# Hybrid HGRN2, RG-LRU and MoE block on one core: moving the convolution's leading product, shortening GELU's argument and reordering the gate matmuls

## What is computed

```python
proj = h @ w_in + b_in
q, f_pre, v, g_out, lru_x, lru_g, gate_hg, gate_lru = split(proj)
y_hg = hgrn2_mixer(q, f_pre, v, g_out, lb, norm_g)          # S_t = diag(f_t) S_{t-1} + (1-f_t) v_t^T, o_t = S_t^T q_t
y_lru = rg_lru(causal_depthwise_conv(lru_x, conv_w, conv_b), ...) * gelu(lru_g)
merged = sigmoid(gate_hg) * y_hg + sigmoid(gate_lru) * y_lru
h = layer_norm(alpha * h + merged @ w_out)
h = layer_norm(alpha * h + shared_swiglu(h) + routed_experts(h))   # 64 experts, 6 per token
```

## Time and profile before

| | us |
|---|---|
| median of three runs | 1241.81 |
| lowest and highest | 1236.87, 1247.73 |
| profiled execution, its own time | 1246.69 |
| its span, first to last instruction | 1244.5 |
| PE busy | 1142.2 (92%) |
| PE's weight loads busy (beside the matmuls) | 737.9 (59%) |
| DVE busy | 764.5 (61%) |
| ACT busy | 426.9 (34%) |
| POOL busy | 205.3 (17%) |
| mean granted clock of TensorE | 0.977 |

### The profile page before, as it was taken

How to read it: one execution, slowest core, us unless ns; L and a number is a source line. 1 busy time by engine, 2 the same in 40 slices (tenths; PEclk the granted TensorE clock), 3 DMA queues, 4 the chain that set the end, 5 groups by cost and what they waited for, 6 DMA issues and landing times. The chain is left out here.

```text
span 1244.5 us, 17998 instructions
## 1 busy us (share of the span) xinstructions
PE 1142.2 (92%) x6336; PEld 737.9 (59%) x6336; DVE 764.5 (61%) x1276; ACT 426.9 (34%) x667; POOL 205.3 (17%) x109
## 2 busy tenths in 40 slices
PE   4999999999999999999899889989999989999991
PEld 4888878787879797456344444444444444444440
DVE  7748687878687777754535445544455535555558
ACT  6656564746565565011022121111111212112220
POOL 1524242433333333000000000000000000000000
PEclk9999999999999999999999899999999989999996
DMA  5303030303031203093669899998999989999923
GB/s 222 121 21 121 20 139 0 139 0 139 0 139 38 101 34 135 28 391 148 240 259 421 358 414 374 396 403 359 418 384 383 422 354 422 412 417 405 410 101 118
DMA packets 48291, 292.57 MB, mean 235 GB/s; under 512 B 7680, under 2 KB 9088, under 8 KB 16528
## 3 DMA queue, kind: packets, MB, share of 16 engines
q1 hardware_dynamic: 42944, 272.92, 54.1%
q0 software_dynamic: 5328, 19.40, 4.3%
HBM read 288.10 MB, written 4.19 MB: 235 GB/s over the span
## 5 line engine op out<-in xcount | busy, mean ns | idle before, releaser
L366 PE MATMUL pair<-hT,w_parts 128*128 128x264 f32 (+1 forms) x2112 | 378.3, 339 | 2.8 <-DVE hT L635 2.4
L366 PEld LDWEIGHTS pair<-hT,w_parts 128*128 128x128 f32 x2112 | 321.5, 189 | 49.3 <-issue 5.4
L1276 PE MATMUL pair<-raw,xgT 128*64 128x512 f32 x1088 | 239.2, 592 | 0.0
L1373 DVE TENSOR_TENSOR acc<-acc,pair 128x512 f32<-128x512 f32 x280 | 171.7, 680 | 78.6 <-PE pair L1301 78.5
L216 POOL TENSOR_TENSOR w_parts<-w_raw,w_parts 128x1024 fp32r<-128x1024 f32 x66 | 166.9, 2530 | 316.2 <-ACT w_parts L210 301.1
L1276 PEld LDWEIGHTS pair<-raw,xgT 128*64 128x64 f32 x1088 | 78.2, 137 | 155.2 <-issue 155.2
L850 POOL DMA_INDIRECT xg<-h_rows,idx x37 | 34.8, 942 | 678.1 <-DVE idx L844 678.1
L1309 PE MATMUL pair<-raw,aT 128*64 128x512 f32 x544 | 124.2, 598 | 0.0
L1348 ACT ACTIVATE y_hi<-pair,w_now 128x512 fp32r<-128x512 f32 x70 | 48.1, 687 | 216.3 <-PE pair L1309 215.4
L1300 PE MATMUL pair<-y_hi,ST 128*128 128x512 f32 x280 | 118.1, 422 | 1.6 <-DVE y_lo L1382 1.6
L1364 DVE TENSOR_TENSOR act_a<-act_s,pair 128x256 f32<-128x256 f32 x35 | 14.7, 421 | 169.7 <-ACT act_s L1341 169.7
(11 more groups left out here) (266 smaller groups left out, 1204.4 us busy)
## 6 DMA issues: line engine op xcount, KB each, us to landing
raw<-in_w_gate_up SPq DMA_DIRECT2D x136, 1024.0 KB, 9.8
raw<-in_w_down SPq DMA_DIRECT2D x68, 1024.0 KB, 8.3
w_raw<-in_w_in SPq DMA_DIRECT2D x36, 1024.0 KB, 6.7
first<-in_w_gate_up SPq DMA_DIRECT2D x4, 1024.0 KB, 11.7
xin<-in_x SPq DMA_DIRECT2D x4, 512.0 KB, 5.3
ws_gu<-in_ws_gate_up SPq DMA_DIRECT2D x1, 2048.0 KB, 7.7
h_rows<-acc SPq DMA_DIRECT2D x4, 512.0 KB, 21.1
first<-in_w_down SPq DMA_DIRECT2D x2, 1024.0 KB, 10.1
```

The lines of the kernel that those rows point to most:

```text
L366: last = pe.matmul(o, w[:, n % PARTS, pw, k * P:(k + 1) * P], hT[ph][:, k, of], start=(k == 0 and m == 0), stop=(k == KB - 1 and m == 2))
L1276: last = pe.matmul(GU[half[s], :], xgT[b][:, (KB // 2) * c + k, half[s]], w[s][:, k * 2 * F:(k + 1) * 2 * F], start=(c == 0 and k == 0), s ...
L1373: v.tensor_tensor(part, part, SUM[g % len(SUM)], ALU.add).then_inc(sem("sum_free"), 1)
```

## The change

Three edits in the mixer. ACT makes the first product of the convolution (`w3*x + cb`) right behind `xr`, with a semaphore of its own (`xc_begun`), and DVE adds the other three taps. GELU's argument is `(x^2 + 1/GELU_A) * x`, in a square and one `scalar_tensor_tensor`, and the factor GELU_A goes into the scale of ACT's sigmoid. On PE the transpose of the meta tokens' `k_st` comes first and has a semaphore of its own (`ktm_done`, `ktm_taken`), the two wide gate matmuls come ahead of the two narrow ones, and only the narrow ones wait for `ktm_taken`.

```diff
--- before.py
+++ after.py
@@ -278,7 +278,7 @@
         of_half = lambda bank: bank[:, 0:TT * CHUNK].rearrange("p (t s) -> p t s", t=TT)
         chunked = lambda t: t.rearrange("p (c s) -> p c s", c=NCH)
 
-        per_head = ("f_done q_done v_done vt_done x_done o_done l_done hg_done lru_done kt_done ri_done sc_done "
+        per_head = ("f_done q_done v_done vt_done x_done o_done l_done hg_done lru_done ktm_done kt_done ri_done sc_done "
                     "kv_done out_done rms_done").split()
         pe_sem = {n: sem("pe_" + n) for n in per_head}
 
@@ -391,14 +391,17 @@
 
 
                     pe.wait_ge(sem("kst_ready"), j + 1)
+                    pe.transpose(B7[0:META, 256:384], k_st[:, 0:META], ident[:]).then_inc(pe_sem["ktm_done"], 1)
                     for t in range(TT):
-                        pe.transpose(B4[:, t * P:(t + 1) * P], k_st[:, META + t * P:META + (t + 1) * P], ident[:])
-                    pe.transpose(B7[0:META, 256:384], k_st[:, 0:META], ident[:]).then_inc(pe_sem["kt_done"], 1)
+                        last = pe.transpose(B4[:, t * P:(t + 1) * P], k_st[:, META + t * P:META + (t + 1) * P], ident[:])
+                    last.then_inc(pe_sem["kt_done"], 1)
                     pe.wait_ge(sem("xc_ready"), j + 1)
                     pe.wait_ge(sem(f"lw_here_{s}"), 16 * r + 16)
-                    pe.wait_ge(sem("kt_taken"), j + 1)
                     for i, bank in enumerate((B5, B6)):
                         pe.matmul(bank[:, 0:T], lw[s][:, i], xc[:, META:TA], start=True, stop=True)
+
+                    pe.wait_ge(sem("ktm_taken"), j + 1)
+                    for i in range(2):
                         last = pe.matmul(B7[:, 32 + 16 * i:48 + 16 * i], lw[s][:, i], xc[:, 0:META],
                                          start=True, stop=True)
                     last.then_inc(pe_sem["ri_done"], 1)
@@ -528,14 +531,18 @@
                     for of, bank in zip(split_at, wide[GX]):
                         last = act.activation(xr[:, 3 + of.start:3 + of.stop], bank[:, 0:TA // 2], ACT.Identity, bias=c(C_BX))
                     last.then_inc(sem("x_taken"), 1)
+                    act.wait_ge(sem("x_taken"), j + 1)
+                    act.activation(xc[:], xr[:, 3:3 + TA], ACT.Identity, scale=c(C_W3), bias=c(C_CB))\
+                       .then_inc(sem("xc_begun"), 1)
                     split_hi(act, j, 7)
                     act.wait_ge(pe_sem["o_done"], j + 1)
                     act.activation(sg[0][:], BV_[:, 0:T], ACT.Silu, bias=c(C_BG)).then_inc(sem("o_taken"), 1)
                     split_hi(act, j + 1, 0)
                     act.wait_ge(pe_sem["l_done"], j + 1)
                     act.activation(gx[:], BQ_[:, 0:T], ACT.Identity, bias=c(C_BL)).then_inc(sem("l_taken"), 1)
+                    act.wait_ge(pe_sem["ktm_done"], j + 1)
+                    act.activation(kTm[:], B7[0:META, 256:384], ACT.Copy).then_inc(sem("ktm_taken"), 1)
                     act.wait_ge(pe_sem["kt_done"], j + 1)
-                    act.activation(kTm[:], B7[0:META, 256:384], ACT.Copy)
                     act.activation(kT[:].rearrange("p t c -> p (t c)"), B4[:, 0:T], ACT.Copy).then_inc(sem("kt_taken"), 1)
                     split_hi(act, j + 1, 1)
 
@@ -546,7 +553,7 @@
                     act.activation(ii[:, META:TA], B6[:, 0:T], ACT.Sigmoid, bias=c(C_BI)).then_inc(sem("ri_taken"), 1)
                     act.wait_ge(sem("ri_taken"), j + 2)
                     act.wait_ge(sem("gelu_arg"), j + 1)
-                    act.activation(gt[:], gt[:], ACT.Sigmoid, scale=GELU_B).then_inc(sem("gelu_sig"), 1)
+                    act.activation(gt[:], gt[:], ACT.Sigmoid, scale=GELU_A * GELU_B).then_inc(sem("gelu_sig"), 1)
                     act.activation(la[:], rr[:], ACT.Exp, scale=own[s][:, 2:3])
                     act.activation(pp[:], rr[:], ACT.Tanh, scale=own[s][:, 3:4]).then_inc(sem("a_ready"), 1)
                     act.wait_ge(pe_sem["hg_done"], j + 1)
@@ -565,7 +572,7 @@
 
         @block.vector
         def _(v):
-            N = 38
+            N = 36
             st0 = Steps(v, sem("dve2_step"))
             st0.add(v.memset(ones[:], 1.0))
             st0.add(v.memset(k_in[:], 0.0))
@@ -682,8 +689,7 @@
                         else:
                             ins.then_inc(sem("qk_ready"), 1)
 
-                    v.wait_ge(sem("x_taken"), j + 1)
-                    st(v.tensor_scalar(xc[:], xr[:, 3:3 + TA], c(C_W3), c(C_CB), ALU.mult, ALU.add))
+                    v.wait_ge(sem("xc_begun"), j + 1)
                     for i in range(3):
                         ins = v.scalar_tensor_tensor(xc[:], xr[:, i:i + TA], c(C_W0 + i), xc[:], ALU.mult, ALU.add)
                         if i < 2:
@@ -692,8 +698,8 @@
                             ins.then_inc(sem("xc_ready"), 1)
                     v.wait_ge(sem("l_taken"), j + 2)
                     st(v.tensor_tensor(gt[:], gx[:], gx[:], ALU.mult))
-                    st(v.tensor_scalar(gt[:], gt[:], GELU_A, 1.0, ALU.mult, ALU.add))
-                    v.tensor_tensor(gt[:], gt[:], gx[:], ALU.mult).then_inc(sem("gelu_arg"), 1)
+                    v.scalar_tensor_tensor(gt[:], gt[:], 1.0 / GELU_A, gx[:], ALU.add, ALU.mult)\
+                     .then_inc(sem("gelu_arg"), 1)
                     v.wait_ge(pe_sem["sc_done"], j + 1)
                     v.tensor_tensor(sc[:], B4[:, 0:TT * CHUNK].rearrange("p (t c) -> p t c", t=TT),
                                     cmask[:].rearrange("p (a c) -> p a c", a=1).broadcast_to([P, TT, CHUNK]),
```

## The result

Four executions of the changed kernel took 1218.3 to 1231.0 us, median 1225.22, against 1239.5 for four of the kernel before: ratio 0.988, 95% interval [0.983, 0.993]. I had said 1237.1 with 1228.5 to 1245. The measured median lies under the range, and the gain, 14.3 us, is three times the forecast 4.7. Two further series of the same kernel gave 0.997 [0.994, 0.999] and 0.998 [0.994, 1.001]. Both facts need an explanation. Ratios and means here leave out, for every kernel alike, the executions more than 1.5% above the fastest of their series (10 of 92 of the kernel before, one of 27 of the changed kernel) and one execution of the changed kernel that took 1958.4 us at a mean granted clock of 0.556.

What follows compares the result with a forecast made beforehand. The mixer was taken to be bound by PE, with 12.3 us of waits at the wide gate matmuls. Terms 4.2 + 0.9 - 0.4 = 4.7 us, from the median 1241.81, gave 1237.1 us; eight-in-ten range 1228.5 to 1245.

Steps and rivals of the forecast that it cites:

- The port: DVE's convolution taps and POOL's splits keep each other out of SBUF; two waits remain, xc only 0.6 us sooner per head.
- Part 1: Convolution's first product moved from DVE to ACT: xc 0.6 us sooner in seven heads, 4.2 us saved.
- Part 3: PE's order at the gates: 0.9 us gained in head 0, 0.4 us lost in all on grouped narrow matmuls.
- Part 2: GELU's argument in two operations: gelu_arg 0.3 to 3 us sooner, worth 0 at the end of the mixer.
- The sum: Whole kernel: 4.2 + 0.9 - 0.4 = 4.7 us saved, from the median 1241.81 to 1237.1 us.
- The range: Eight-in-ten range for the whole kernel's time, 1228.5 to 1245 us; the forecast's own range was 1234 to 1240.
- Rival B: PE's wait at the wide gate matmuls closes wholly: all 12.3 us go, less 0.4, giving 1229.9 us; chance 0.12.
- Rival C: Grouped narrow gate matmuls make TensorE's clock fall in six more mixer heads: 9.6 us lost, giving 1246.7 us; chance 0.08.

Runs made afterwards that it cites:

- the late-split kernel: The changed kernel with ACT's split of group 7 put behind the Silu of O, so POOL asks later; ratio to before 0.994 [0.991, 0.997].
- the one with both splits late: The late-split kernel with the split of the next head's group 1 also put behind the gates' sigmoids; ratio to before 0.988 [0.984, 0.993].

## Why the prediction was right and wrong

**The port: right, part by part.** In head 1's old times (2.38 us added) the forecast against the trace: POOL's first request 115.28, measured 115.28; the second 118.23, measured 118.23; the ACTIVATE 0.82 us, measured 0.83; `xc` ready at 122.25, measured 113.20 + 6.55 + 2.38 = 122.13. GELU's operation just ahead of POOL: 122.76 against 123.10, and it took 0.69. By this the wait at L401 should have been 1.0 us and was 0.9 and 0.8 in turn, 6.1 in seven heads. ("Almost no data from HBM" was loosely read: the mixer moves 76 GB/s. But no wait of PE in its heads ends on a DMA.) The rule of the Trainium skill, "SBUF — State Buffer", section "Who interferes with whom", that two-input operations are kept out like two-port ones, is borne out by 2792 ns of median in L694, and by the late-split kernel, where the same line takes at most 771 ns in all heads.

**Part 1's size** was a little low: 7 x 0.6 = 4.2 stood for what came to (11.4 - 6.1) = 5.3 together with part 3. The product alone gave 4.7 before `kT` stopped it.

**Part 2** worth nothing: shown by itself.

**Part 3**: 0.9 forecast for head 0 and 0.4 lost on the narrow matmuls. Measured 0.95 less 0.26, and nothing lost. I had named `ri_taken` as the next wait and put it at a gain of over 1 us; in head 0, with 0.95, it was there already. The wait for `kT` also mattered more than I said: without part 3 the seven heads would have stopped at 0.95 each.

**The sum**: 4.7 forecast, 6.0 in the waits, 6.5 +- 1.1 in time over all executions.

**The range is the step that failed**: "For eight in ten the range has to take in most of B and of C and the spread of the three runs: 1228.5 to 1245". It went by three executions of the kernel before and their median of 1241.8; over 82 the mean is 1238.3. Under it lies a term that I put at nothing without a reason: "The expert stage behind it is PE's and the DMA's and is not edited; it starts when PE ends the mixer, so a microsecond saved there is saved at the end". What is saved does arrive there, but the stretch behind the mixer is not the same each time: 706.4 to 723.8 us over fourteen profiles, 721.0 in the profile before and 712.7 in the one after. I treated the clock only as a rival inside the mixer, C, whose falls I counted as a loss, while most of the falls are in the expert stage, six in the profile before, two of them double; and the wait for gathered rows I didn't consider. The profile before was itself a slow draw, 8 us over the mean of its kernel, and its mean granted clock of 0.977 lies under those of all 92 others on record (0.978 to 0.989).

With what is known now the forecast would be 1238.3 - 4.7 = 1233.6 us, and a median of four executions, of which each scatters by 4.9, is uncertain by nearly 3. Eight in ten would then be about 1230 to 1237, so the 1225.2 of the first four lies outside even so. That part stays open.

**Rival B did not happen**, though its number, 1229.9, is the nearest to the first measurement. Whoever judged by the time alone would have taken it for shown.

**Rival C** was right in what it feared and wrong in its reason. The grouping of the narrow matmuls did not bring more falls: one or none in the heads of the changed kernel's three profiles, two in both of the kernel before. The place it named is the place where they come, with the grouping and without it.

## What to carry to other kernels

When DVE is slow on an operation, look at POOL in the same microseconds: an operation that is replaced gives back its own work, but the wait goes over to the next one with two SBUF inputs; moving POOL's request past the critical operations took it away here, and cost no instruction. A gain of half a per cent can't be read from four executions when the clock's draw moves each by as much: compare the waits in the trace, in the edited stage and in those behind it, and the mean granted clock with the time. And when a bottleneck engine is filled up, look at what its short operations do to its clock.

## What was not expected of the hardware

In the mixer the clock's fall depends on what PE does within a few microseconds. With scores and state update in one run, all 16 falls in 88 heads begin 4.9 to 5.5 us behind the start of the gates' matmuls, whether PE had waited 1.6 us ahead of them, as in the kernel before, or not at all, as in the one with both splits late. With six wide matmuls set between, there is none in 24 heads. A run of this kind doesn't always bring a fall: two profiles have none in the loop. What decides it, the runs don't say.

The same code behind the mixer takes 706.4 to 723.8 us by the number of falls and by PE's wait for the gathered rows, and which it will be is chance as far as these runs show: they gave no kernel that changed it. And one execution of twelve in the third series took 1958.4 us at a mean clock of 0.556, of which there is no trace.
